# The first expert prepared inside the mixing block, lists built from the token columns alone, and a hint on the layer loop's back edge

## The reference, cut to what matters

```
for l in range(2):
    mix = hybrid_mixer(x, ...)                       # three kinds of attention, then @ w_out
    x = layer_norm(ALPHA * x + mix, ln1_g, ln1_b)    # x1
    scores = sigmoid(x @ router_w)
    _, idx = top_k(scores + router_bias, 8)
    gates = scores[idx] / sum * 2.5
    for each expert e: y = (silu(h @ w1[e]) * (h @ w3[e])) @ w2[e], h = x1 rows of its tokens
    shared = (silu(x @ sw1) * (x @ sw3)) @ sw2
    x = layer_norm(ALPHA * x + routed + shared, ln2_g, ln2_b)
```

## Time and profile before

| | us |
|---|---|
| median of 3 runs | 2211.39 (2210.4 to 2211.49) |
| profiled execution | 2211.91 |
| its span | 2210.1 |
| TensorE busy | 2095.2 (95%) |
| VectorE busy | 1658.3 (75%) |
| ScalarE busy | 1410.4 (64%) |
| GpSimd busy | 590.3 (27%) |

### The profile page before, as it was taken

The page is one execution under the profiler, slowest core; times in us unless marked ns, Lnnn a source line. Parts: engine busy times, 40 slices in busy tenths (PEclk is TensorE's granted clock), DMA queues, the critical chain, the costliest instruction groups (busy, mean ns, idle before and its releaser), DMA issues. The chain is left out here.

```text
span 2210.1 us, 32222 instructions
## 1 busy us (share of the span) xinstructions
PE 2095.2 (95%) x10968; PEld 1670.7 (76%) x10968; DVE 1658.3 (75%) x2403; ACT 1410.4 (64%) x1762; POOL 590.3 (27%) x336
## 2 busy tenths in 40 slices
PE   6999989799999999999889999897999999999996
PEld 4779878588888888887376888776888888888862
DVE  2485453699999999998346834546999999999955
ACT  3442752388888888887044337415888888888851
POOL 0010300034444444433011021001444444444320
PEclk9999999899999999999999999998999999999999
DMA  5312213499999999996741140254999999999938
GB/s 199 96 30 61 122 66 146 177 344 380 390 377 367 379 384 388 381 377 237 305 136 59 49 161 2 75 238 151 379 380 381 386 378 376 379 377 376 378 145 358
DMA packets 136062, 572.87 MB, mean 259 GB/s; under 512 B 32356, under 2 KB 58468, under 8 KB 82712
## 3 DMA queue, kind: packets, MB, share of 16 engines
q1 hardware_dynamic: 99096, 504.37, 59.6%
q0 software_dynamic: 36864, 67.19, 8.1%
HBM read 560.41 MB, written 78.14 MB: 289 GB/s over the span
## 5 line engine op out<-in xcount | busy, mean ns | idle before, releaser
L1384 PE MATMUL ps_sum<-w_hi,rowsT_hi 128*128 128x512 f32 x1024 | 426.2, 416 | 15.4 <-DVE rowsT_lo L1494 15.4
L1386 PE MATMUL ps_sum<-w_hi,rowsT_lo 128*128 128x512 f32 x1024 | 406.1, 397 | 0.0
L1324 POOL DMA_INDIRECT rows<-x_rows,index x122 | 290.9, 2385 | 168.6 <-DVE index L1469 161.0
L1482 DVE TENSOR_TENSOR w_lo<-w,w_hi 128x2048 fp32r<-128x2048 f32 x128 | 292.6, 2287 | 46.9 <-ACT w_hi L1534 46.9
L1482 DVE TENSOR_TENSOR w_next_lo<-w_next,w_hi 128x2048 fp32r<-128x2048 f32 x128 | 292.7, 2286 | 20.1 <-ACT w_hi L1534 20.1
L1534 ACT CAST w_hi<-w 128x2048 fp32r<-128x2048 f32 x128 | 245.2, 1917 | 39.0 <-PE ps_sum L1386 18.8
L1534 ACT CAST w_hi<-w_next 128x2048 fp32r<-128x2048 f32 x128 | 245.0, 1914 | 12.4 <-PE ps_sum L1386 7.1
L1384 PEld LDWEIGHTS ps_sum<-w_hi,rowsT_hi 128*128 128x128 f32 x1024 | 195.5, 191 | 51.1 <-issue 17.4
L1386 PEld LDWEIGHTS ps_sum<-w_hi,rowsT_lo 128*128 128x128 f32 x1024 | 193.9, 189 | 44.4
L1409 PE MATMUL ps_sum<-w_hi,hiddenT_hi 128*128 128x512 f32 x512 | 211.3, 413 | 3.9 <-DVE hiddenT_lo L1501 3.9
L1385 PE MATMUL ps_sum<-w_next_lo,rowsT_hi 128*128 128x512 f32 x512 | 202.7, 396 | 0.0
(11 more groups left out here) (256 smaller groups left out, 4667.1 us busy)
## 6 DMA issues: line engine op xcount, KB each, us to landing
w_next<-exp_w SPq DMA_DIRECT2D x192, 1024.0 KB, 8.7
w<-exp_w SPq DMA_DIRECT2D x128, 1024.0 KB, 9.3
w_first<-exp_w SPq DMA_DIRECT2D x32, 1024.0 KB, 6.5
w_last<-exp_w SPq DMA_DIRECT2D x32, 1024.0 KB, 6.6
wbuf<-w_in SPq DMA_DIRECT2D x16, 1024.0 KB, 5.5
got<-y_rows SPq DMA_DIRECT2D x8, 2048.0 KB, 20.8
got<-y_rows SPq DMA_DIRECT2D x16, 1024.0 KB, 24.1
w_out_sb<-w_out SPq DMA_DIRECT2D x2, 4096.0 KB, 19.3
```

Source lines behind the costliest of these rows:

```text
L1324: pool.indirect_dma_start(rows[0:CAP, x.slot, :], None, d["x1_rows"], bass.IndirectOffsetOnAxis(ap=index[0:CAP, x.step, 0:1], axis=0), bou ...
L1384: pe.matmul(ps_up[b][0:CAP], hi, w_hi, start=(k == 0), stop=False)
L1386: mm = pe.matmul(ps_up[b][0:CAP], lo, w_hi, start=False, stop=(k == KD - 1))
L1482: dve.tensor_tensor(w13_lo[x.slot][:, :, k, :], w13[x.slot][:, :, k, :], w13_hi[:, :, k, :].bitcast(F32), ALU.subtract).then_inc(S["up_lo_ ...
```

## The change

Four things are changed.

1. In the mix block the last router group comes after the first two of eight steps of a shared product, and the other shared products are cut into pieces, with other work between them.
2. The one-hots of experts 0 to 2 are made at once after `posm`, ahead of the table's columns of places and gates. `pick` takes a range of columns, and is done twice for each of the three experts: first over the token columns alone (`pick_token`, `tokens`), then over places and gates (`gates`). The third one-hot lies in a buffer of its own (`junk`). The casts of the table are given to ScalarE. The lap count is made ahead of the second picks.
3. The first expert's preparation is done in the mix block: ScalarE casts its up weights (a semaphore of their own, `first_up_in`, tells that they have landed), VectorE subtracts (`lower_up`), TensorE turns its gathered rows into the PSUM of the router and the counts, ScalarE casts and VectorE subtracts them. The high weights and the two parts of the turned rows are views at the low end of the memory over `oT_hi`, `r`, `gain1` and `shift1`, which are not used any more by then; the expert block holds the place with `first_expert`. The expert block starts without these steps, and its waits count one less.
4. The layer loop is made with `hint_back_edge=True`. [...]

In the diff, `pick(k, values)` is the old pick over those columns; `tokens(k)` sums the first pair of columns into the list of token numbers, `gates(k)` the others; `less(q)` subtracts a cast part from the gate; `lower_up(half)` is the subtraction of half the up weights of expert 0. Its core, with the engine's name ahead of each part:

```diff
@@ _mix_and_route, TensorE @@
-                shared_up(2, 0, early)
+                shared_up(2, 0, early, range(2))
                 router(NT - 1)
-                shared_up(1, 0, early)
+                shared_up(2, 0, early, range(2, KD))
+                shared_up(1, 0, early, range(3))
...
                 mm.then_inc(S["pos_made"], 1)
-                shared_up(3, 0, early)
+                shared_up(1, 0, early, range(3, KD))
+                pick_token(0)
+                shared_up(3, 0, early, range(2))
+                pick_token(1)
+                shared_up(3, 0, early, range(2, 4))
+                pick_token(2)
+                shared_up(3, 0, early, range(4, KD))
                 for q in (0, 2):
                     shared_up(q, early, SEQ).then_inc(S["up_made"], 1)
                 pe.wait_ge(S["tables"], 1)
-                pick(0)
-                pick(1)
-                for q in (1, 3):
-                    shared_up(q, early, SEQ).then_inc(S["up_made"], 1)
-                pick(2)
+                pick(0, range(DEST, PART))
+                pick(1, range(DEST, PART))
+                shared_up(1, early, SEQ).then_inc(S["up_made"], 1)
+                pick(2, range(DEST, PART))
+                shared_up(3, early, SEQ).then_inc(S["up_made"], 1)
+                pe.wait_ge(S["rows0_in"], 16)
+                pe.wait_ge(S["counted"], 1)
+                for k in range(KD):
+                    mm = pe.transpose(turned[k // HALF][:, (k % HALF) * P:(k % HALF + 1) * P], sb["rows"][0:CAP, 0, k::KD], ident)
+                mm.then_inc(S["first_turned"], 1)
@@ _mix_and_route, ScalarE, after the exponential @@
+                act.wait_ge(S["first_up_in"], 32)
...
+                for half in range(2):
+                    k = slice(HALF * half, HALF * half + HALF)
+                    act.copy(w13_hi[:, :, k, :], sb["w13"][0][:, :, k, :]).then_inc(S["up_hi"], 1)
+                for q in range(3):
+                    act.wait_ge(S["gate_left"], q + 1)
+                    act.copy(parts[:, :, :, GATES + q], gate[:]).then_inc(S["parts_cast"], 1)
+                act.wait_ge(S["place_ready"], 1)
+                act.copy(parts[:, :, :, DEST], place[:]).then_inc(S["dest_cast"], 1)
...
+                act.wait_ge(S["first_turned"], 1)
+                for half in range(2):
+                    act.copy(rowsT_hi[:, HALF * half:HALF * half + HALF, :].rearrange("p k c -> p (k c)"), turned[half]
@@ _mix_and_route, VectorE, after posm (in place of hots, indices, gated in turn) @@
+                for k in range(FIRST):
+                    hots(k)
+                for k in range(FIRST):
+                    tokens(k)
+                less(0)
...
+                less(1)
...
+                o.then_inc(S["place_ready"], 1)
                 step(dve.tensor_reduce(cnt[:, 0:1], ps_c[:, 0:NE], AX.X, ALU.max))
...
+                dve.wait_ge(S["dest_cast"], 1)
+                dve.wait_ge(S["parts_cast"], 3)
+                dve.tensor_tensor(parts[:, :, :, DEST_LOW], place[:], parts[:, :, :, DEST], ALU.subtract).then_inc(S["tables"], 1)
+                lower_up(0)
+                gates(0)
+                gates(1)
+                hots(FIRST)
+                lower_up(1)
+                gated(0)
+                gates(2)
...
+                gated(1)
+                for half in range(2):
+                    dve.wait_ge(S["first_hi"], half + 1)
+                    k = slice(HALF * half, HALF * half + HALF)
+                    dve.tensor_tensor(rowsT_lo[:, k, :].rearrange("p k c -> p (k c)"), turned[half],
@@ _experts @@
-                turn_rows(Turn(0, 0))
...
-                up_lo(Turn(0, 0), 0)
-                up_lo(Turn(0, 0), 1)
-                rows_lo(Turn(0, 0))
...
-                up_hi(Turn(0, 0), 0)
-                up_hi(Turn(0, 0), 1)
-                rows_hi(Turn(0, 0))
@@ trunk @@
-        with nc.Fori(0, DEPTH) as l:
+        with nc.Fori(0, DEPTH, hint_back_edge=True) as l:
```

More of the change, by code:

```diff
@@ L917, in _ @@
                 sp.wait_ge(S["x1_out"], 64)
[L918 removed]
+                sp.wait_ge(S["ahead_in"], EARLY - 32)
             @block.gpsimd
@@ L972, in router, with shared_up @@
                     mm.then_inc(S["logits_made"], 1)
-                def shared_up(q, first, last):
-                    for k in range(KD):
+                def shared_up(q, first, last, ks=range(KD)):
+                    for k in ks:
                         mm = pe.matmul(up_bank[q][:, first:last], w13[:, q // 2, k, (q % 2) * P:(q % 2 + 1) * P],
@@ L990, in _, with pick, pick_token @@
                         router(t - 2)
-                def pick(k):
+                picks = 0
+                def pick(k, values):
+                    nonlocal picks
+                    if picks >= 2:
+                        pe.wait_ge(S["index_ready"], picks - 1)
+                    out = flat_x[0:CAP, (picks % 2) * 512:(picks % 2) * 512 + len(values)]
+                    values = slice(values[0], values[-1] + 1)
+                    for t in range(NT):
+                        pe.matmul(out, hots_at[k][:, t, :], sb["parts"][:, t, k, values], start=(t == 0), stop=False)
+                    pe.matmul(out, absent[:, 0:CAP], absent[:, CAP + values.start:CAP + values.stop], start=False, stop=True
+                              ).then_inc(S["picked_made"], 1)
+                    picks += 1
+                def pick_token(k):
                     pe.wait_ge(S["hot_ready"], k + 1)
                     pe.wait_ge(S["tokens"], 3)
[L996 to L1002, removed]
+                    pick(k, range(IDX, DEST))
                 pe.wait_ge(S["shared_in"], 32)
@@ L1171, in gated, with lower_up @@
                     dve.tensor_tensor(act_out[:, m, :], up_bank[m + 2], act_out[:, m, :], ALU.mult).then_inc(S["gated"], 1)
-                hots(0)
-                hots(1)
-                indices(0)
-                hots(2)
-                indices(1)
-                hots(3)
-                gated(0)
-                indices(2)
+                def lower_up(half):
+                    k = slice(HALF * half, HALF * half + HALF)
+                    dve.wait_ge(S["up_hi"], half + 1)
+                    dve.tensor_tensor(w13_lo[:, :, k, :], sb["w13"][0][:, :, k, :], w13_hi[:, :, k, :].bitcast(F32),
+                                      ALU.subtract).then_inc(S["up_lo"], 1)
+                for k in range(FIRST):
[3 more added lines that the diff above has]
+                less(0)
+                for t in range(NT):
+                    o = dve.tensor_tensor_scan(place[:, t, :], mask[:, t, :], mask[:, t, :], 0.0, ALU.add, ALU.max)
+                step(o)
+                less(1)
+                for t in range(NT):
+                    o = dve.tensor_scalar(place[:, t, :], place[:, t, :], sb["row"][:, PLACE_AT + t:PLACE_AT + t + 1], None, ALU.add)
+                o.then_inc(S["place_ready"], 1)
                 step(dve.tensor_reduce(cnt[:, 0:1], ps_c[:, 0:NE], AX.X, ALU.max))
@@ L1256 @@
 EARLY = (2 * SLOTS + EARLY_DOWN) * 16
+FIRST_EXPERT = 2 * KD * FF + 2 * KD * CAP
 def _experts(nc, d, sb, l, last):
```

115 lines of the change are left out of this document (67 added, 48 removed).

## The result

The changed kernel has a median of 2195.22 us (2192.84 to 2195.94, 4 runs) against 2210.89 (2209.07 to 2211.49, 4 runs): ratio 0.9929, interval 0.9917 to 0.9941. That is 15.7 us (0.7%) less. The forecast was 20.7 less than 2211.4, so 2190.7, in a range of 2187.5 to 2199. The time lies in the range, with some three quarters of the gain that I had worked out; it lies between the times of rivals A (2193.9) and B (2196.8) and nearer to both than to my forecast, so it can't tell the three apart.

What follows compares the result with a forecast made beforehand. TensorE was taken to bound the expert stage, so an earlier start ends it earlier. 2211.9 - 17.5 (experts' start, two layers) - 3.2 (hint) = 2191.2, and 0.5 less for the median: 2190.7 us, range 2187.5 to 2199.

Steps and rivals of the forecast that it cites:

- Rival A: Back edge of the layer loop: the hint does nothing, so 2193.9 us; chance 0.21.
- Rival B: Mix block's end: VectorE, or a row landing late, ends it about 3 us later than forecast, so 2196.8 us; chance 0.19.
- What bounds the kernel: Expert stage: TensorE bounds it, not DMA, so a stage that starts earlier ends earlier by as much.
- rival D: Second expert: held by something that doesn't move, so the 17.5 us come back as a wait; 2208 to 2211; chance 0.03.
- Part 1: Mix block: last router group after 4 of 16 shared-product matmuls, 3.87 us earlier; alone it ends nothing earlier.
- Part 2: Mix block: lists from token columns alone; gathers issued near 396.5, 398.3 and 400.6, so they leave the path.
- Part 3: VectorE's chain in the mix: savings and added work balanced, ending at 411.7 against 410.99; ends 411.1 and 414.7.
- Sum 411.7: Mix block: forecast time at which VectorE's chain, and so the block, ends; 410.99 before.
- Part 4: Start of the experts: first up product at 414.3 against 423.05, 8.75 us per layer, 17.5 for two layers.
- Part 5: Back edge of the layer loop: the hint brings the body's first instructions in time, gaining 3.2 us.
- C: Rival for the whole kernel: the changed kernel is slower; chance 0.04.
- the 2186 for both: Start of the experts: full clock there on both layers, a gain above the ends, 2186 us; 0.03 left for it.

Runs made afterwards that it cites:

- c_order: Changed kernel with table work moved into VectorE's waits for token picks and the first rows turned ahead of TensorE's last two products: 2186.88 us, ratio .9895.
- a_dvecast: Changed kernel with the four casts of the tables on VectorE again instead of ScalarE: 2195.79 us, ratio .9932.
- a_nohint: Changed kernel with the layer loop's back-edge hint taken out: 2196.03 us, ratio .9925.
- b_hint: Kernel before the change, given the layer loop's back-edge hint alone: 2208.40 us, ratio .9986.
- c_both: c_order with semaphores also cleared in runs of consecutive numbers: 2187.36 us, ratio .9897.
- c_both_again: The same kernel as c_both, timed in more rounds on a second chip session: 2186.62 us, ratio .9890.
- c_warm: c_both with two more TensorE products, whose result nothing reads, behind its last one in the mix: 2187.19 us, ratio .9901.

## Why the prediction was right or wrong

**What bounds the kernel, and rival D.** Right. Earlier starts of the expert stage were kept to the end: the second expert starts 7.04 us earlier in layer 0 (434.42 in the kernel before, 427.38 here), more than the 6.56 of the first. The extra 0.5 is clock, since the stage began with 4.2 us at a granted clock of 0.50 and not 5.3 (a matmul of the product starts 0.43 us after the one before there, and 0.23 after it from then on). Rival D is out.

**Part 1.** Right: TensorE's first instruction of layer 1 to VectorE's first routing one fell from 355.4 to 351.3, 4.1 for my 3.87. In layer 0 VectorE's first routing instruction came 2.99 earlier (387.26 to 384.27), so this layer's mix ran 0.9 late. Both are within what the blocks ahead vary by: that stretch took 350.1 to 352.4 us in the 22 layers of the eleven profiles with the router moved (mean 351.2), and 354.5 to 355.4 in the four layers without (mean 354.9). So the move is worth 3.7 us, and the 0.9 needs no cause in this change.

**Part 2.** Right: gathers at 397.50, 399.02 and 400.32, for 396.5, 398.3 and 400.6, with the layer 0.9 late, and the lists off the path (the drains above). The dearer issue that I weighed did not come: the second and third of each layer took 0.99 us, the first 1.22 and 1.10, not 2.45. The record shows when it does come. In the expert stage of the changed kernel 117 of 122 gathers start while VectorE is in a 128x2048 subtraction, and each ends 0.87 to 0.91 us after that subtraction's end, 2.39 to 2.88 us in all. One of them, GpSimd and then VectorE:

```profile
445.09 2.43 POOL L1401 DMA_INDIRECT rows<-x_rows,index  x1 [0.92 <-DVE index L1545]
```

```profile
444.36 2.28 DVE L1558 TENSOR_TENSOR w_next_lo<-w_next,w_hi 128x2048 fp32r<-128x2048 f32 x1
```

In the mix block no such subtraction was under way: beside its gathers VectorE had small reductions, a 128x256 subtraction and scans. c_order tests it harder. There VectorE starts the weight subtraction 0.04 us after its third gather has started, and the gather still takes 0.99:

```profile
399.66 0.99 POOL L932 DMA_INDIRECT rows<-x_rows,index  x1 [0.31 <-issue]
```

```profile
399.70 4.71 DVE L1223 TENSOR_TENSOR w_lo<-w,w_hi 128x2048 fp32r<-128x2048 f32 x2
```

I had weighed the 2.45 us for all gathers beside VectorE, which was too wide: in these traces the price is paid where a weight subtraction is already under way (2.39 to 2.88 us), and neither the small instructions nor a subtraction that started later lengthened a gather (0.99). Landing took 5.2 (3.7 before), within the double that I had allowed, and the slack took it.

**Part 3.** Here the sum was off: "Sum 411.7", measured 413.91. 0.9 of the 2.2 is layer 0's late start, which leaves 1.3. In layer 1 the gain on R is 39.7 - 32.0 = 7.6 of 8.75, so 1.1 is missing there. The step that failed is "The casts on ScalarE cost nothing as long as it is idle". I took idleness for speed. They take 1.34 us there, not 0.74, and stand in a relay with VectorE's subtractions: VectorE waits 0.69 and 0.82 for them, where I had 0. The second wait was to be covered by the lap count (1.2 us); it wasn't, because ScalarE had the last gate cast from 402.18 and took the place cast only behind it, until 404.66, when VectorE had ended the lap count at 403.87. The three pick waits were 3.38 instead of 3.0. That makes 1.9 us of waits too few. VectorE's own work, which I had at 2.9 us more than before, was 2.3 more, so 0.6 came back and 1.3 is left. My sign of error for this part, that VectorE idles over 1 us after the tables, did not show: the waits are ahead of the tables, and each under 1 us. And a_dvecast shows what the move was worth: against casts on VectorE the -3.1 that I had booked comes to 0.1 us, partly since the first cast would have fallen into the 1.71 of waiting for the positions anyway. Rival B had the right mechanism, a tight relay, at 3 us where it was 1.3. c_order shows that some 2.5 us of such waiting can be had back by the order of the work alone.

**Part 4.** The barrier step was right: VectorE's end to first up product 2.58 us, forecast 2.6. VectorE ended the block, as forecast; TensorE, which I had ending at 409.7, ended at 411.4, with its 0.48 us of wait for the tables in it. TensorE's standstill was 4.98, where 409.7 and 414.1 had left 4.4, and the first up product began at a granted clock of 0.50 as in the kernel before (its first matmul 0.77 us, 0.76 before).

**Part 5.** The hint gave what I had booked for it: 3.2 us, seen by itself in a_nohint, and 2.9 in b_hint. That it would was my guess, since no row had a hinted edge; and the 0.05 us that I had for the hint itself came from no row either; it takes 0.04 to 0.07. Rival A is out: the branch takes 0.39 us in place of 3.50. VectorE's first instruction of the layer comes 0.53 us behind GpSimd's, where I had 0.3 at most; it was 3.48 before. What the late start is made of, and how the hint removes it, no run shows; they show that it goes although a whole layer lies between the hint and the branch. A slower kernel (C, 0.04) is out too: with the hint alone the expert stages would have to be longer, and b_hint's are 639.5 us, for 641.7 and 640.9 before. But the edge gained 2.02 us and not 3.2: the hint gave 2.9 on the kernel before, and 0.84 went to the clearing over 146 numbers. I had counted the new waits, and not the new semaphores. The same clear of 0.83 us comes once more at the end of layer 1; from the second norm's first load to the kernel's end it was 57.3 us, 57.4 before, so that one does not show in the sum.

Together: 6.56 + 7.88 + 2.02 = 16.5 of my 20.7. Missing are 2.19 in layer 0 and 0.87 in layer 1, both before the experts, and 1.2 at the edge (0.84 of it the clear). The time came into the range since the range held a loss of this size; the mechanism was right in parts 1, 2 and 4, the size of the hint's gain in part 5, and part 3 had the casts' price wrong.

**What the medians hide.** The expert stage of kernels whose expert code is the same took 637.9 to 643.2 us, and it goes with the clock of its first 24 us. Windows of that length, which I chose (us; busy by engine; granted clock; DMA share; GB/s), c_order's in layer 0 and then the changed kernel's in layers 0 and 1:

```profile
413.37:437.37 24.00, 21.45 (x115) 17.76 (x113) 18.94 (x23) 17.10 (x16) 5.03 (x3) 1.00 0.60 222
```

```profile
416.49:440.49 24.00, 21.79 (x101) 17.78 (x100) 15.63 (x19) 14.13 (x14) 1.98 (x2) 0.84 0.47 162
1496.42:1520.42 24.00, 21.46 (x110) 17.69 (x108) 17.50 (x20) 15.78 (x15) 3.73 (x3) 0.94 0.53 193
```

At 1.00 TensorE fits 115 products in, at 0.84 only 101, and the stages are 638.1 and 640.9 us. The sizes fit: at .80 the window lacks 24 x 0.20 = 4.8 us of full clock, and the two stages at .80 are 5.2 us longer than the three at 1.00. I had bounded this at 2.4 us per layer (the 2186 for both), for twelve matmuls at 0.43 us a start in place of 0.23; it is up to 5. Whether the shorter standstill of c_order makes full clock likelier is open. The profiles of c_order, c_both and c_both_again show 1.00 in three of six stages, and the nine of kernels without the reorder in none of 18; by the first product alone (0.48 us at full clock, 0.77 at half) six of the eight stages of the four reordered profiles started at full clock, and one of the 18 others, a_dvecast's in layer 1 after 4.79 us of standstill. But c_both_again stood still just as long as c_order (3.30) and began at a granted clock of 0.50. And a start at full clock did not keep it: c_both's layer 0 and both of c_warm, after 1.98 and 1.84 of standstill, started so and fell later, to .86 and .93.

## What to carry to other kernels

Work moved to an idle engine is not free (here 1.34 us a cast in place of 0.74): price it at that engine's own duration for that operation, and draw the relay (who waits, then who waits for him) before booking the saving. An edit's new semaphores can cost in a place that the diff doesn't touch (here 0.84 us at a layer's end), so look at what is cleared, and over what range. And when two kernels differ by less than the noise of a long common stage (here 637.9 to 643.2 us), compare the stretches that the change touches, not the medians.

## What the runs showed of the hardware that was not expected

- A hint on this loop's back edge worked across a body of one whole layer with an inner loop in it: TensorE's taken branch 0.39 us for 3.50, edge 2.9 to 3.2 us shorter; it costs 38 to 65 ns per engine and pass.
- Clearing a range of semaphores costs by the range: 0.83 us and a drain of 0.26 for 146 numbers (the changed kernel), 0.16 and 0.09 for 24 (the kernel before).
- An indirect gather that GpSimd starts while VectorE is in a 128x2048 subtraction ends 0.87 to 0.91 us after that subtraction (117 of 117 in the changed kernel); one that starts 0.04 us ahead of it takes 0.99 in all (c_order).
- A cast of 128x256 float32 to strided bf16 takes 1.34 us on ScalarE and 0.74 on VectorE.
- After the same standstill of 3.3 us TensorE started once at a granted clock of 1.00 (0.40 us a matmul of 128x512, c_order) and once at 0.50 (0.63, c_both_again). The two stages together are 2.9 us shorter in c_order, more than some of the edits tested gave (0.6 to 0.7 us at the edge for the clearing in runs).
